# Causal mask of two attention layers: added by VectorE in the accumulator, in place of TensorE products of identity and mask

## What is computed

```python
# differential attention, 8 heads, two components c per head
s = jnp.einsum('bqhcd,bkhcd->bhcqk', q_i.astype(jnp.float32), k32)
mask = key_pos[None, :] <= q_pos[:, None]
s = jnp.where(mask, s, -jnp.inf)
p = jax.nn.softmax(s, axis=-1)
a = p[:, :, 0] - lam * p[:, :, 1]

# latent attention, 8 heads
scores = (jnp.einsum('bqhd,bkhd->bhqk', qn, k_nope)
          + jnp.einsum('bqhr,bkr->bhqk', qr, k_rope)).astype(jnp.float32) * scale
scores = jnp.where(key_idx[None, :] <= q_idx[:, None], scores, -jnp.inf)
```

## Time and profile before

| what | value |
|---|---|
| device time, three runs | 2648.56, 2649.01, 2652.90 us; median 2649.01 |
| the profiled execution's own time | 2647.77 us |
| its span | 2645.9 us |
| busy, share of the span | PE 97%, PEld 82%, DVE 51%, ACT 41%, POOL 44% |
| chain of work that ended last | PE 91%, DVE 5%, ACT 2%, POOL 1% |
| differential attention (heads 0 to 7) | about 40 to 249 us |
| one head of heads 1 to 6 | 25.9 us |
| latent attention (heads 0 to 7) | about 2107 to 2215 us |
| mask matmuls | 64 at L1529, 32 at L2235 |

### The profile page before, as it was taken

One profiled execution on the slowest core, in us unless ns is written; L12 is line 12 of the kernel. 1 busy time (PEld: TensorE's weight loads), 2 busy tenths in 40 slices (PEclk: granted clock), 3 DMA queues, 4 the chain that ended last, 5 costly groups with the idle time before them and its releaser, 6 DMA issues.

```text
span 2645.9 us, 32320 instructions
## 1 busy us (share of the span) xinstructions
PE 2571.1 (97%) x13086; PEld 2163.6 (82%) x13086; DVE 1360.7 (51%) x2097; ACT 1094.1 (41%) x1880; POOL 1170.1 (44%) x634
## 2 busy tenths in 40 slices
PE   7999999999999999998999999999999999999997
PEld 6887988888789888887787777888888888888886
DVE  6776550533444604426766575562562775651644
ACT  5554531334224413324554454542332654542432
POOL 3332574345355743443334233544446425544443
PEclk9999999999999999999999999899999999999998
DMA  5221333332333333322222222223333113223322
GB/s 155 62 69 50 95 96 96 96 96 73 103 96 86 99 99 100 96 74 72 72 64 80 72 72 70 67 87 105 98 89 100 43 43 88 80 83 113 100 84 68
DMA packets 436005, 224.26 MB, mean 85 GB/s; under 512 B 14864, under 2 KB 433936, under 8 KB 435856
## 3 DMA queue, kind: packets, MB, share of 16 engines
q1 hardware_dynamic: 435856, 222.18, 29.4%
HBM read 219.01 MB, written 2.10 MB: 84 GB/s over the span
## 4 chain that ended last, share of the span: by engine, by line
PE 91%; DVE 5%; ACT 2%; POOL 1%; issue 1%; DMA 0%; SPq 0%; DVEq 0%; POOLq 0%; ACTq 0%
PE ps L521 29%; PE ps L523 28%; PE ps L522 28%; PE ps L2646 1%; PE ps L2632 1%; PE ps L1499 1%; PE ps L1420 1%; DVE acc L1478 0%; DVE acc L1472 0%; PE ps L1522 0%; DMA xT<-in_xT 0%; PE ps L2634 0%; ACT tmp L1656 0%; POOL sm L1813 0%; PE ps L2671 0%
## 5 line engine op out<-in xcount | busy, mean ns | idle before, releaser
L495 POOL TENSOR_TENSOR wl<-stg,wh 128x1024 fp32r<-128x1024 f32 (+4 forms) x447 | 1002.8, 2250 | 1238.5 <-ACT wh L487 1231.3
L521 PE MATMUL ps<-hh,wh 128*128 128x512 f32 (+2 forms) x2292 | 862.3, 376 | 37.6 <-POOL wl L495 13.6
L523 PE MATMUL ps<-hh,wl 128*128 128x512 f32 (+2 forms) x2292 | 851.0, 371 | 0.0
L522 PE MATMUL ps<-hl,wh 128*128 128x512 f32 (+2 forms) x2292 | 850.6, 371 | 0.0
L487 ACT ACTIVATE wh<-stg 128x1024 fp32r<-128x1024 f32 (+4 forms) x447 | 436.2, 985 | 312.7 <-DMA stg<-in_mlp_w_down 111.1
L521 PEld LDWEIGHTS ps<-hh,wh 128*128 128x128 f32 (+1 forms) x2292 | 434.2, 189 | 116.3 <-issue 23.8
L521 PE MATMUL ps<-bh,wh 128*128 128x512 f32 (+1 forms) x1320 | 493.6, 374 | 2.9 <-DVE bl L1775 1.6
L523 PEld LDWEIGHTS ps<-hh,wl 128*128 128x128 f32 (+1 forms) x2292 | 434.0, 189 | 74.8
L522 PEld LDWEIGHTS ps<-hl,wh 128*128 128x128 f32 (+1 forms) x2292 | 434.7, 190 | 71.3 <-issue 1.0
L523 PE MATMUL ps<-bh,wl 128*128 128x512 f32 (+1 forms) x1320 | 489.8, 371 | 0.0
L522 PE MATMUL ps<-bl,wh 128*128 128x512 f32 (+1 forms) x1320 | 489.6, 371 | 0.0
(11 more groups left out here) (320 smaller groups left out, 2666.0 us busy)
## 6 DMA issues: line engine op xcount, KB each, us to landing
stg<-in_ffn_up SPq DMA_DIRECT2D x88, 512.0 KB, 3.8
stg<-in_mlp_w_up SPq DMA_DIRECT2D x64, 512.0 KB, 4.1
stg<-in_mlp_w_down SPq DMA_DIRECT2D x64, 512.0 KB, 4.0
stg<-in_ssd_in_proj SPq DMA_DIRECT2D x48, 512.0 KB, 3.9
stg<-in_attn_w_qkv SPq DMA_DIRECT2D x24, 512.0 KB, 4.0
stg<-in_conv_w_in SPq DMA_DIRECT2D x24, 512.0 KB, 3.8
stg<-in_ffn_down SPq DMA_DIRECT2D x32, 384.0 KB, 3.3
stg<-in_ffn_down SPq DMA_DIRECT2D x32, 320.0 KB, 3.1
```

What stands on the lines that cost most here:

```text
L495: pool.tensor_tensor(wl[:, slab.slot, w], stg[:, slab.slot, w], wh[:, slab.slot, w].bitcast(F32), ALU.subtract).then_inc(s.lo_done, 1)
L521: pe.matmul(po, lh, rh, start=start, stop=False)
L522: pe.matmul(po, lh, rl, start=False, stop=False)
L523: return pe.matmul(po, ll, rh, start=False, stop=stop)
```

## The change

PE's mask matmuls are gone. The last of the three score products of each block and component now ends the accumulation and signals `scores_done`. DVE adds the mask to the last 128 columns of the block in place in PSUM, signals a new semaphore `masked`, and takes the maximum behind it. In differential attention both components' adds go ahead of both maxima; in latent attention add and maximum follow one another. The mask operand is the same rounded tile in SBUF, read as fp32.

```diff
@@ DiffAttention.score_products
-                    pe.matmul(ps[:, bank, off:off + (b + 1) * P], q[rows, self.Q_, b * P:(b + 1) * P],
-                              k[rows, self.K_, 0:(b + 1) * P], start=q is bh and k is bh, stop=False,
-                              skip_group_check=True)
-
-        def score_masks(self, pe, h, blocks):
-            for c, b in blocks:
-                bank, off = score_place(h, c, b)
-                pe.matmul(ps[:, bank, off + b * P:off + (b + 1) * P], ident_r, mask_r, start=False, stop=True,
-                          skip_group_check=True).then_inc(s.scores_done, 1)
+                    end = pe.matmul(ps[:, bank, off:off + (b + 1) * P], q[rows, self.Q_, b * P:(b + 1) * P],
+                                    k[rows, self.K_, 0:(b + 1) * P], start=q is bh and k is bh, stop=q is bl,
+                                    skip_group_check=True)
+                    if q is bl:
+                        end.then_inc(s.scores_done, 1)
...
@@ DiffAttention.scores
-            self.score_masks(pe, h, ((0, 3), (1, 3), (0, 2), (1, 2)))
             self.score_products(pe, h, 0)
             if h > 0:
                 pe.wait_ge(s.o_norm, h)
             if 0 < h < HEADS - 1:
                 self.score_products(pe, h, 1)
-                self.score_masks(pe, h, ((0, 0), (1, 0), (0, 1), (1, 1)))
             else:
-                self.score_masks(pe, h, ((0, 0), (1, 0)))
                 for c in range(2):
                     if c:
                         pe.wait_ge(s.scores_done, 8 * h + 7)
                     self.score_products(pe, h, 1, (c,))
-                    self.score_masks(pe, h, ((c, 1),))
@@ DiffAttention.softmax
                 for c in range(2):
                     bank, off = score_place(h, c, b)
                     dve.wait_ge(s.scores_done, 8 * h + SCORED[b][c])
+                    last = ps[:, bank, off + b * P:off + (b + 1) * P]
+                    dve.tensor_tensor(last, last, mask_r.bitcast(F32), ALU.add).then_inc(s.masked, 1)
+                for c in range(2):
+                    bank, off = score_place(h, c, b)
+                    dve.wait_ge(s.masked, 8 * h + 2 * n + c + 1)
                     dve.reduce_max(mx[:, 2 * n + c:2 * n + c + 1], ps[:, bank, off:off + (b + 1) * P],
                                    axis=AX_X).then_inc(s.max_done, 1)
@@ LatentAttention.scores
-                pe.matmul(ps[:, bank, off + n - P:off + n], ident_r, mask_r, start=False, stop=False)
-
@@ LatentAttention.softmax
                 dve.wait_ge(s.m_scores, 4 * h + self.SCORED[b])
+                last = ps[:, bank, off + b * P:off + (b + 1) * P]
+                dve.tensor_tensor(last, last, mask_r.bitcast(F32), ALU.add).then_inc(s.masked, 1)
+                dve.wait_ge(s.masked, 8 * HEADS + 4 * h + n + 1)
                 dve.reduce_max(mx[:, n:n + 1], ps[:, bank, off:off + (b + 1) * P], axis=AX_X).then_inc(s.m_max, 1)
```

More of the change, by code:

```diff
@@ L246, in program @@
         scores_done = new("scores_done")
+        masked = new("masked")
         max_done = new("max_done")
```

## The result

The changed kernel takes 2662.49 us (median of 5 runs, 2660.53 to 2666.38) against 2649.01 us: a ratio of 1.0051, 95% interval 1.0037 to 1.0064. It is slower, as forecast, but by 13.5 us where 6.5 were forecast, and half a microsecond outside the range. The profiled execution has a span of 2658.7 us, 12.8 more than before's 2645.9.

A forecast was written before the change was run, and what follows sets the result against it. PE bound 91% of the span, but in heads 1 to 6 PE's and DVE/ACT's branches ended together. 7.2 + 0.8 - 0.3 - 1.2 = +6.5 on the median 2649.01 gave 2655.5 us, range 2650.5 to 2662.

The forecast's parts named there:

- The price of an add: DVE's 128-column add in place in PSUM: 0.20 us of engine time, upper bound 0.26; one block 0.40.
- three of four blocks count: Heads 1 to 6: three blocks of adds precede the third `negmax` ACT needs, so exponentials end 1.2 us later.
- the removal from PE gains nothing: Heads 1 to 6: PE's removed masks stood ahead of waits for `o_norm` or V's low parts; gain taken as nothing.
- Head 7: Differential attention's last head: PE saves some masks but then has to wait for DVE's last combination; -0.3 us.
- The first rival: DVE instructions in line cost their whole duration, 0.28 us an add; +10.6 us, 2659.6; chance 0.08.
- Rival 2: POOL's L495 catches DVE's earlier L1728 of block 0; needs adds above 0.70 us a block; +3.6, 2659.1; chance 0.05.
- rival 3: Heads 1 to 6: PE's clock falls, its branch 1.7 us longer and later by 0.5; +3, 2658.5; chance 0.12.
- Head 0: Differential attention's first head: POOL swallows block 3's adds, blocks 2 and 0 count at 0.4 us each; +0.8.
- Latent attention: Fewer PE masks against DVE's serial adds and maxima: together -1.2 us, between -3.5 and +1.
- the three steps that were to gain 0.4 each: Latent attention, odd heads: PE's arrival is 0.91 us behind DVE's end, so nearly all is kept; three times -0.4 = -1.2.
- the last one: Latent attention, head 7: PE already waits 0.9 us for L2392, which comes 0.6 later; +0.6.
- that of the even heads: Latent attention, even heads: PE's next scores gain 0.1 to 0.2 us; heads 0 and 6 wait already; four heads -0.6.

The follow-up runs named there:

- filled kernel: The changed kernel with PE's score products of block 0 done three times and of block 1 twice in heads 1 to 6; 2667.35 us, ratio 1.0064.
- the kernel before with the split: The kernel before with POOL's roundings under attention and three slabs behind it each issued as four instructions of 256 columns; 2650.22 us, ratio 1.0003.

## Why the prediction was wrong

**What held.** The price of an add: 0.20 a step, 0.39 to 0.40 a block. That three of four blocks count: +1.19 at the exponentials in heads 1 to 6, shown alone in five heads of 27.07. That the removal from PE gains nothing in those heads: they are 25.89 at full clock with no mask at all. Head 7: -0.20 for -0.3. The first rival, DVE instructions costing their whole 0.28, is out: two adds take 0.49.

**What failed, by size.** Of the 6.3 us by which the profiled pair misses the sum, head 0 has 3.9, heads 1 to 6 have 2.5, latent attention 0.9 and head 7 0.1; what lies elsewhere gives 1.1 back. In both parts of differential attention it is the same step: I moved DVE's instructions against POOL's and held that no further one of them would be caught, and that PE's clock would stay.

**Rival 2 was put at a chance of 0.05 by a wrong reading.** It said that POOL could catch an earlier L1728 only if the gap of 0.70 were used up. The gap was measured to the wrong instruction. The one behind it, L1730 of the same block, is caught as well; it ended 0.02 ahead of POOL's start. What shrinks the gap by any amount brings the collision. Its price was put at 0.6 a head, and is 1.5: in the forecast the caught instruction's delay was set against PE's arrival only, where it costs 0.3; in fact PE's further work and POOL's next roundings move behind it, and the third rounding holds the variance, for 1.2. With it a head costs 2.7, not 1.2. In the changed kernel itself that is one head of six; the other five escape it by the low clock. The Trainium skill, page "GPSIMD Engine Reference", section "1. Specifications", says that its SBUF interfaces are shared with VectorE, with contention for DVE instructions in a 2-port mode or with two SBUF inputs. The trace agrees: L1728, with two inputs in SBUF, was held. L1726, with one, was held too; whether it ran in such a mode the trace doesn't tell. And instructions that read PSUM ran through, as these of head 3 after, three in 1.62 in the middle of a rounding:

```profile
144.31 2.53 POOL L496 TENSOR_TENSOR wl<-stg,wh 128x1024 fp32r<-128x1024 f32 x1 [2.99 <-ACT wh L488]
144.76 1.62 DVE L1735 TENSOR_TENSOR bl<-ps,bh 128x512 fp32r<-128x512 f32 x3 [0.18 <-ACT bh L1644]
```

**The clock, rival 3, happened in five of six heads**, at a chance of 0.12 and a price of 0.5 a head beyond the sum; a head comes to +1.45 with it, 0.26 beyond it. What spoke against it, "none of the six has such a fall now", was no argument: those heads had the 0.5 us of masks that the change takes out of PE's wait. Each of the two rivals was priced as if it came alone and in all six heads. They came in the same kernel, in different heads: one makes 28.6, the other 27.35, and no head was left at the 27.07 that I forecast. (The filled kernel has two heads with both, also of 28.6.)

**Head 0** was put at +0.8 and is +4.7, the largest term that was missed. I let one POOL instruction catch one DVE instruction, as before, and left PE and POOL where they were. PE's earlier second projection brings ACT's second slab forward, so that POOL's two roundings meet and hold two instructions (most of the 2.7 in the first column above), and behind 6 us of standing still PE runs at the low clock (2.05). That POOL is what makes head 0 longer is shown: with POOL's instructions short the change makes it shorter, 25.28 for 27.02.

**Latent attention** was put at -1.2 and is -0.26. Measured between the transposes of one head and the next, the three steps that were to gain 0.4 each gained 0.35, and the last one lost 0.65 where 0.6 was forecast (PE waits 1.6 at L1500 in head 7). The term that failed is that of the even heads, -0.6: two of them gained 0.05 and 0.07, one nothing, and head 0 lost 0.26, where PE now waits 0.6 for L2391 and had not waited before. The two halves priced apart are -3.0 for the products and +2.1 for the adds.

The terms in order, forecast and measured in the profiled pair: heads 1 to 6 +7.2, +9.7; head 0 +0.8, +4.7; head 7 -0.3, -0.2; latent -1.2, -0.26; elsewhere 0, -1.1.

What makes the clock low in one head and not in the next isn't settled. A wait of PE for `out_scaled` stood ahead of each such stretch in heads 1 to 6, of 1.06 or more in all cases but one, 0.73 in head 6 of the kernel before with the split. But waits of 1.08 and 1.09 in the kernel without masks had none behind them, nor had one of 1.60 in the filled one. That the missing masks bring the falls is likely (none in heads 1 to 6 before, four in the kernel without masks), but not shown apart from the waits.

## What to carry to other kernels

Before work is added to an engine in a balanced loop, list for every instruction behind it how far it is from the next long instruction of the engine that shares its memory path, its own end included, not just its start. A gap of 0.02 us is no gap. Work that looks free on TensorE, because it sits ahead of a wait, may be part of what keeps its clock up; price its removal at both clock levels, and look at the wait that it leaves. And where two engines' branches end together, an early arrival on one is not a gain but a wait, with its own consequences.

## What the runs showed of the hardware

- DVE held off by POOL waits until the POOL instruction in hand has ended and gets in ahead of the next: 2.52 us for an instruction of 0.35 under one of 1024 columns, 0.85 under one of 256, and 2.15 and 2.33 in two instructions under two that follow each other.
- Splitting a rounding of 1024 columns in four costs POOL 0.3 to 0.7 us (2.8 to 3.2 for 2.4 to 2.6).
- An add in place in PSUM of 128 columns takes 0.28 to 0.29 us and occupies DVE for 0.20 when another follows that doesn't depend on it.
- The clock was granted at half for 3.4 us in heads of the changed kernel in which the longest wait of PE for another engine was 1.1 us, and stayed full in others with the same wait. The Trainium skill, page "TensorE: Matmul & The Clock Gate", section "HAM oscillation — how this bites in real kernels", puts such falls down to longer gaps in TensorE's work; this trace doesn't agree, it has them behind these short ones.
- A halved clock can shorten a head, 27.35 in place of 28.6, where it moves POOL's start by 0.2 us, past DVE's instruction.
